# The gated delta rule of a two-block model: packed 64x64 blocks, worked beside the projections

## The reference, cut to what matters

```
q, k, v = split(silu(causal_dwconv(concat(q, k, v), conv_w)))       # 4 taps
beta = sigmoid(b);  g = -exp(a_log) * softplus(a + dt_bias)
q = l2norm(q) * 128 ** -0.5;  k = l2norm(k)
gcum = cumsum of g in each chunk of 64;  decay[t, s] = exp(gcum[t] - gcum[s]) for s <= t, else 0
N = -(strictly lower part of (beta k) k^T * decay)
T = I + N;  P = N
for _ in range(5):  P = P @ P;  T = T + T @ P
w = T @ (beta k exp(gcum));  u = T @ (beta v)
attn = q k^T * decay;  q_g = q exp(gcum);  k_g = k exp(gcum[last] - gcum)
for each chunk c (in order):                                        # the scan
    v_new = u - w @ S;  o = q_g @ S + attn @ v_new;  S = S * exp(gcum[last]) + k_g^T @ v_new
y_a = rmsnorm(o) * norm_w * silu(z)
```

## Time and profile before

| what | value |
|---|---|
| median of three runs | 2964.35 us |
| the profiled execution's own time | 2963.22 us |
| its span, first to last instruction | 2961.3 us |
| TensorE busy | 2835.7 us, 96% of the span |
| VectorE (DVE) busy | 1564.7 us, 53% |
| ScalarE (ACT) busy | 841.1 us, 28% |
| GpSimd (POOL) busy | 206.2 us, 7% |
| granted TensorE clock, mean | 0.983 of full speed |

### The profile page before, as it was taken

How to read it: one execution, slowest core, us unless ns; L and a number is a source line. 1 busy time by engine, 2 the same in 40 slices (tenths; PEclk the granted TensorE clock), 3 DMA queues, 4 the chain that set the end, 5 groups by cost and what they waited for, 6 DMA issues and landing times.

```text
span 2961.3 us, 31843 instructions
## 1 busy us (share of the span) xinstructions
PE 2835.7 (96%) x12912; PEld 2303.7 (78%) x12912; DVE 1564.7 (53%) x1824; ACT 841.1 (28%) x870; POOL 206.2 (7%) x182
## 2 busy tenths in 40 slices
PE   7999998899999997899989999999999999999997
PEld 6777776688777776778777888888888888888887
DVE  6456454683543567562465545445454544445458
ACT  4335244552421232222232122212222122222122
POOL 3003000160000000001040000000000000000004
PEclk9999999999999999899999999999999999999999
DMA  5224311242222220022232222222222222222232
GB/s 196 72 71 171 121 58 57 102 173 100 92 87 85 75 90 35 1 111 88 99 128 86 100 99 87 100 100 100 92 95 100 100 100 88 97 101 100 97 147 85
DMA packets 44379, 287.52 MB, mean 97 GB/s; under 512 B 5136, under 2 KB 9360, under 8 KB 10432
## 3 DMA queue, kind: packets, MB, share of 16 engines
q1 hardware_dynamic: 39616, 260.06, 24.0%
q0 software_dynamic: 4320, 24.85, 2.2%
q10 hardware_dynamic: 288, 0.43, 0.0%
HBM read 268.54 MB, written 16.78 MB: 96 GB/s over the span
## 4 chain that ended last, share of the span: by engine, by line
PE 87%; DVE 8%; ACT 3%; issue 1%; POOL 0%; DMA 0%; DVEq 0%; SPq 0%; ACTq 0%; POOLq 0%
PE ps L1135 10%; PE ps L1137 10%; PE ps L1136 10%; PE ps L610 9%; PE ps L612 9%; PE ps L611 9%; PE ps L1153 5%; PE ps L1152 5%; PE ps L1151 5%; PE ps L1059 2%; PE ps L1061 2%; PE ps L1060 2%; PE ps L949 1%; DVE w_lo L1708 1%; ACT w_hi L1205 1%
## 5 line engine op out<-in xcount | busy, mean ns | idle before, releaser
L1708 DVE TENSOR_TENSOR w_lo<-raw,w_hi 128x2048 fp32r<-128x2048 f32 x228 | 529.3, 2322 | 538.4 <-ACT w_hi L1205 528.6
L1205 ACT ACTIVATE w_hi<-raw 128x2048 fp32r<-128x2048 f32 x227 | 434.5, 1915 | 1224.6 <-PE ps L1137 478.1
L610 PE MATMUL ps<-h_hi,w_hi 128*128 128x512 f32 x1216 | 495.2, 407 | 17.3 <-DVE h_lo L1713 15.5
L1135 PE MATMUL ps<-h_hi,w_hi 128*128 128x512 f32 x1280 | 499.7, 390 | 6.5 <-DVE w_lo L1708 4.1
L1137 PE MATMUL ps<-h_hi,w_lo 128*128 128x512 f32 x1280 | 499.0, 390 | 0.0
L1136 PE MATMUL ps<-h_lo,w_hi 128*128 128x512 f32 x1280 | 498.9, 390 | 0.0
L612 PE MATMUL ps<-h_hi,w_lo 128*128 128x512 f32 x1216 | 477.1, 392 | 0.0
L611 PE MATMUL ps<-h_lo,w_hi 128*128 128x512 f32 x1216 | 477.0, 392 | 0.0
L610 PEld LDWEIGHTS ps<-h_hi,w_hi 128*128 128x128 f32 x1216 | 230.5, 190 | 74.8 <-issue 26.2
L1135 PEld LDWEIGHTS ps<-h_hi,w_hi 128*128 128x128 f32 x1280 | 241.0, 188 | 58.3 <-DVE w_lo L1708 4.5
L1137 PEld LDWEIGHTS ps<-h_hi,w_lo 128*128 128x128 f32 x1280 | 240.9, 188 | 50.3
(11 more groups left out here) (408 smaller groups left out, 3136.5 us busy)
## 6 DMA issues: line engine op xcount, KB each, us to landing
raw<-weights SPq DMA_DIRECT2D x232, 1024.0 KB, 4.8
x_spill<-X POOLq DMA_DIRECT2D x8, 1024.0 KB, 7.1
X<-x_in SPq DMA_DIRECT2D x4, 1024.0 KB, 10.8
x_res<-x_in SPq DMA_DIRECT2D x4, 1024.0 KB, 7.4
x<-X POOLq DMA_DIRECT2D x4, 1024.0 KB, 4.6
x_res<-x SPq DMA_DIRECT2D x4, 1024.0 KB, 7.8
X<-x_spill POOLq DMA_DIRECT2D x4, 1024.0 KB, 9.4
x_back<-x_spill POOLq DMA_DIRECT2D x4, 1024.0 KB, 9.0
```

The source lines that it names most:

```text
L610: pe.matmul(o, w_hi[:, s % 2, w], h_hi[:, t, :], start=(t == 0), stop=False)
L1135: pe.matmul(o, w_hi[:, s % 2, w], h_hi[:, t, :], start=(t == 0), stop=False)
L1205: A(w_hi[:, slot, :], raw[:, slot, :], ACT.Copy).then_inc(w_hi_ready, 1)
L1708: V.tensor_tensor(w_lo[:, slot, :], raw[:, slot, :], w_hi[:, slot, :].bitcast(F32), ALU.subtract).then_inc(w_ready, 1)
```

## The change

- The 16 units take a `beat`, and one generator `delta_rule` issues the whole preparation on TensorE between the k-tiles of v (beats 64 to 95) and of z (96 to 127). The copies and elementwise steps move into the lists of ACT and DVE beside these units. No loop over `pair` stands behind the projections any more.
- Head i and head i + 2 are packed: the 64 tokens of a chunk of one lie on partitions 0 to 63, those of the other on 64 to 127. A product over blocks is 16 matmuls of 64x64 by 64x64 for two heads (j = 0 and j = 1 on the two halves of the rows), all in one bank (`packed`). Silu writes q, k and v in that packed order.
- The transposed powers are computed by a product of their own in place of a transpose, and both are copied by ACT.
- The l2 norms are not applied to the tiles. The sums are taken per token (`l2_sums`: 32 matmuls with one moving column), and the factors of q and k go into per-token vectors (`token_factors`), which are spread over rows with an identity as moving operand (`spread`).
- The scan handles four heads in 64-row halves of bank 4 (w by state), banks 5 and 6 (k_g by v_new), makes outputs per chunk of 64 tokens, and multiplies by a copy of attn that is zero in the other head's half. POOL zeroes it after the last unit, and ACT copies into it. Silu of z moves behind ACT's rounding of eight tiles in the scan.

The core of the diff on TensorE:

```
             def turn_ba():
-                for tt in range(4):
-                    mm = pe.transpose(ps[:, 5, 8 * tt:8 * tt + 8], ba_rows[:, 128 * tt:128 * tt + 128], ident[0:8, 0:8])
+                for c in range(8):
+                    for j in range(2):
+                        mm = pe.matmul(ps[64 * j:64 * j + 64, 5, 4 * c:4 * c + 4], ba_rows[:, 64 * c:64 * c + 64], ...)
+            def packed(o, lhs, rhs):
+                for c in range(8):
+                    x = slice(64 * c, 64 * c + 64)
+                    for j in range(2):
+                        r = slice(64 * j, 64 * j + 64)
+                        mm = pe.matmul(o[r, x], lhs[r, x], rhs[r, x], start=True, stop=True)
+            def delta_rule(beat):
+                yield from beat.until(68)
+                sum_gates()
+                yield from beat.until(75)
+                pe.wait_ge(sem("g_sums_read"), 1)
+                for i in range(2):
+                    spread(ps[:, 4 + i, :], g_sums, i).then_inc(full[4 + i], 1)
+                yield from beat.until(84)
+                l2_sums(1)
...
+                for it in range(5):
+                    for i in range(2):
+                        yield from beat.until(97 + 4 * it + i)
+                        pe.wait_ge(read[6 + i], C_PT + it - 1)
+                        pe.wait_ge(read[4 + i], F_P + 2 * it - 1)
+                        packed(ps[:, 4 + i, :], nt_pow[:, i, :], n_pow[:, i, :]).then_inc(full[4 + i], 1)
+                        if it < 4:
+                            packed(ps[:, 6 + i, :], n_pow[:, i, :], nt_pow[:, i, :]).then_inc(full[6 + i], 1)
...
+                    for i in range(2):
+                        yield from beat.until(99 + 4 * it + i)
+                        pe.wait_ge(sem("inv_ready"), i + 1)
+                        pe.wait_ge(read[4 + i], F_INV + 2 * it - 1)
+                        packed(ps[:, 4 + i, :], n_pow[:, i, :], inv_t[:, i, :]).then_inc(full[4 + i], 1)
...
             for n in range(4):
                 for s in range(4):
-                    project_unit(U_QKVZ, G_QKVZ, n, s, 32)
+                    project_unit(U_QKVZ, G_QKVZ, n, s, 32, beat=beat)
...
-            for pair in range(2):
...
+            def scan_output(c, h):
+                o = ps[:, 7 if c // 2 % 2 else 0, 128 * h + 64 * (c % 2):128 * h + 64 * (c % 2) + 64]
+                pe.matmul(o, v_new[:, c % 2, 128 * (h % 2):128 * (h % 2) + 128], attn_z[:, h, 64 * c:64 * c + 64], start=True, stop=False)
+                pe.matmul(o, state[:, c % N_STATES, hs], tokens_at(Q_T, h % 2, c)[:, 64 * (h // 2):64 * (h // 2) + 64], start=False, stop=True)
```

On ACT and DVE, cut to what stands beside which unit:

```
                     if (n, s) == (2, 1):
+                        silu_conv(1)
+                        l2_squares(1)
+                        exp_decay()
+                        take_l2()
+                    if (n, s) == (3, 0):
+                        take_powers(0)
+                        take_powers(1)
+                    if (n, s) == (3, 1):
+                        take_powers(2)
+                        take_powers(3)
+                        silu_conv(2)
...
+                    if (n, s) == (2, 2):
+                        token_factors()
+                        first_powers()
...
                     if (n, s) == (3, 0):
                         dve.wait_ge(bank_free, G_QKVZ + 6 + 2)
+                        conv_taps(2, (0,))
+                        add_power(0)
+                        conv_taps(2, (1,))
+                        add_power(1)
```

More of the change, by code:

```diff
@@ L451, in two_blocks_kernel @@
         dve_order, act_order, pool_order = sem("dve_order"), sem("act_order"), sem("pool_order")
+        full = {b: sem(f"bank{b}_full") for b in range(4, 8)}
+        read = {b: sem(f"bank{b}_read") for b in range(4, 8)}
         block = ctx.enter_context(nc.Block())
@@ new lines, in products, with turn_blocks @@
+            def products(o, a, b, i):
+                for c in range(8):
+                    for j in range(2):
+                        r = slice(64 * j, 64 * j + 64)
+                        mm = pe.matmul(o[r, 64 * c:64 * c + 64], tokens_at(a, i, c)[:, r], tokens_at(b, i, c)[:, r],
+                                       start=True, stop=True)
+                return mm
+            def turn_blocks(b, base, i, half):
+                for c in range(4 * half, 4 * half + 4):
+                    mm = turn(ps[:, b, 128 * (c % 4):128 * (c % 4) + 128], tokens_at(base, i, c))
+                mm.then_inc(full[b], 1)
@@ L936, in _ @@
                         pe.wait_ge(sem("group_root"), 3)
[L937 to L950, removed]
@@ L952, in _ @@
-            for pair in range(2):
[L953 to L1010, removed]
[L1011 to L1018 removed]
+                        l2_sums(0)
@@ new lines, in take_w_and_u @@
+            def take_w_and_u():
+                for i, (b0, use) in enumerate(((6, C_W), (4, F_W))):
+                    for j in range(2):
+                        act.wait_ge(full[b0 + j], use)
+                        A(w_t[:, 2 * i + j, :], ps[:, b0 + j, :], ACT.Copy).then_inc(read[b0 + j], 1)
+                for i, (b0, use) in enumerate(((6, C_U), (4, F_U))):
+                    for half in range(2):
+                        act.wait_ge(full[b0 + half], use)
+                        A(proj[:, V_T + i + 2 * half, PAD:], ps[:, b0 + half, :], ACT.Copy).then_inc(read[b0 + half], 1)
@@ new lines, in take_k @@
+            def take_k(i):
+                b0, use = ((6, C_K), (4, F_K))[i]
+                for half in range(2):
+                    dve.wait_ge(full[b0], use)
+                    dve.wait_ge(full[b0 + 1], use)
+                    cols = slice(8 * i + 4 * half, 8 * i + 4 * half + 4)
+                    V.tensor_tensor(b128(k_be[:, 2 * i + half, :]), b128(ps[:, b0 + half, :]), bc(be[:, cols], 128), ALU.mult)\
+                     .then_inc(sem("k_taken"), 1)
+                    V.tensor_tensor(b128(proj[:, KEY_T + i + 2 * half, PAD:]), b128(ps[:, b0 + half, :]), bc(kgs[:, cols], 128), ALU.mult)\
+                     .then_inc(read[b0 + half], 1)
```

518 lines of the change are left out of this document (323 added, 195 removed).

## The result

The changed kernel takes 2934.08 us (median of four runs, 2932.28 to 2938.03) against 2964.59 us (four runs, 2963.48 to 2964.89): a ratio of 0.990, 95% interval 0.9882 to 0.9917. The forecast was 2938 us, range 2905 to 2972. The profiled execution took 2934.05 us.

What follows compares the result with a forecast made beforehand. TensorE was taken as the bound, busy 96% of the span with 87% of the chain. Removing preparation, adding its matmuls between k-tiles, a later scan start and a shorter scan: 2963.2 - 104.7 + 84.1 + 2.5 - 6.8 = 2938.3 us, range 2905 to 2972.

Steps and rivals of the forecast that it cites:

- signs for "right": Stage some 84 us longer, no preparation behind it, groups of 1.2 to 1.7 us, scan of 31 us at clock 1.0.
- Stage beside the projections: Preparation's matmuls between k-tiles of the v and z units: 84.1 us added, for 104.7 us of preparation removed.
- narrow group: Group of 16 matmuls, 64 rows, 64 weight columns, N = 64, between k-tiles: 1.4 us each, 36 groups, 50.4 us.
- pair row: First layer's scores: two matmuls on different 64-row halves, a pair started every 0.11 us; taken as the lower bound.
- the wait at beat 68: TensorE waits for DVE's gates soon after the v units begin: 1 us (0 to 3).
- the changes of the array: Switches between split and whole array around groups: 0.1 us each way, 32 places, 6.4 us (3.2 to 6.4).
- Wide groups: Six groups for the spread of q's factor, w and u: 1.9 us each, 11.4 us (10.8 to 25).
- Rival (c): Ten places in the powers each wait 1.5 us for a copy; 15 us return, 2953 us; chance 0.12.
- Rival (a): The two row halves, writing one bank, do not work at once: 2.2 us a group of 16, 2982 us; chance 0.18.
- Rival (b): Row halves overlap fully, 0.9 to 1.0 us a group of 16 between k-tiles: 2910 us; chance 0.20.
- The scan: Scan at full clock with chunks of 3.7 to 4.2 us: 31 us against 37.8, a gain of 6.8 (3 to 9).
- The start of the scan: After the last unit, DVE's tiles, POOL's zeroing and ACT's copies: 3.2 us in place of 0.7, +2.5 (1 to 3).

Runs made afterwards that it cites:

- e5: Changed kernel with each of the 28 groups of the powers issued twice, same products into the same places: 2957.97 us.
- e4: Changed kernel with the 16 matmuls in packed() reordered, all eight of the upper rows first, then all eight of the lower: 2952.27 us.
- e8: Changed kernel with three extra unused matmuls behind the first k_g by v_new alone, the gap before the first chunk left empty: 2917.23 us.
- e2: Changed kernel with POOL's zeroing moved to when unit (3, 2) is done, and ACT's copies into attn_z before it takes w and u: 2930.44 us.
- e7: Changed kernel with two extra unused matmuls before the scan's first chunk alone, zeroing unchanged: 2935.02 us.
- e10: Changed kernel with the l2 sums of q issued two matmuls at a time between the k-tiles at beats 69 to 76: 2937.24 us.
- e1: Changed kernel with ten extra unused matmuls at the scan's start: four before the first chunk, six behind the first k_g by v_new: 2916.11 us.
- e3: Changed kernel with POOL's zeroing early and extra unused matmuls, four before the first chunk and three behind the first k_g by v_new: 2912.63 us.
- e6: Changed kernel with POOL's zeroing early and fewer extra unused matmuls, two before the first chunk, one behind the first k_g by v_new: 2915.02 us.
- e11: Changed kernel with POOL's zeroing early, extra unused matmuls in both gaps (two and two) and the l2 sums of q spread between k-tiles: 2928.60 us.
- e12: Changed kernel with POOL's zeroing early, no filler before the first chunk, two extra unused matmuls behind the first k_g by v_new: 2916.20 us.
- e9: Kernel before the change with five extra unused matmuls in its own gaps around the start of the scan: 2952.33 us.

## Why the prediction was right

The time, the direction and the main mechanism (preparation out, its matmuls between the k-tiles, no waits there) came out as forecast. But two terms were wrong and nearly cancelled, so that the number is within 4 us is luck: against the 2938.3 forecast for the profiled execution, the stage beside the projections cost 15.4 us less, the start of the scan 1.2 less and the scan 18.0 more, and the part behind the stage, where nothing was changed, came out 5.6 shorter. Of the signs for "right" in the prediction, groups of 1.2 to 1.7 us and a scan of 31 us at a clock of 1.0 did not come.

- *Stage beside the projections.* Forecast +84.1, measured +68.7, of which 1.0 had come in ahead of the stage. The step that failed is the price of the narrow group: 1.4 us where it is 0.93, 36 x 0.47 = 17 us. I had taken the middle between the pair row and a pace of issue that no row showed; the pair row's half, 0.9, was near the value. The other misses nearly cancel: the products (4 at 0.93 and not 1.9) cost 4 us less, turning b and a 1.5 less (1.03 us where it was 0.34), the wait at beat 68, forecast at 1 us, did not come; against that the changes of the array cost 0.36 us a place and not 0.2, some 5 more for 32 places, and the clock behind the l2 sums some 3 more.
- *Wide groups*: 1.9 forecast, 1.8 measured.
- *Waits in the powers*: TensorE has none in the trace from 1062 to 1204 us. Rival (c) is out, and e5 shows it from the other side.
- *Rival (a), halves in turn*: out, by e4: a group costs 1.6 to 1.7 us only when it is issued in turn, and even with 28 of them so the stage (318.6) is 5 us shorter than before (323.7).
- *Rival (b), full overlap*, forecast 2910: its price for the groups was right, its time not, because of the scan.
- *The scan*, forecast 31 us at a clock of 1.0, measured 49.0 at 0.5. This step failed outright. I reasoned that TensorE comes out of dense k-tiles, and left out what I had worked out a paragraph above: some 3 us of waits for POOL and ACT at the start, in which TensorE has next to nothing. At the lower level a chunk costs 6.0 us; e8 has 29.0 us for the scan with that gap filled, so the forecast of 31 was near for a clock that stays up.
- *The start of the scan*: the first matmul 1.98 us after the tiles are taken, 2.0 forecast. The second chunk waits 2.89 us, where 1.21 are left in e2 without POOL's zeroing and ACT's copies there: 1.7 us late from these, 1.2 forecast.

Two readings in the prediction are off without weight: it writes 1135.56 for 1135.59 in the 104.7 us, and takes the old l2 sums at 3.5 us, where the next k-tile stands 3.03 us behind their start (the new ones cost 1.5 us more in all, 1.6 forecast).

Sum by measured terms, stage only: -104.7 + 68.7 + 1.3 (the scan's first matmul 1.98 us after the tiles are taken, before 0.69 after u) + 11.2 = -23.5, which is the difference of the low parts.

## What to carry to other kernels

Small products that use half the rows can be issued pairwise on the two halves between the k-tiles of a dense projection at little over half the price, also into one bank if the partitions differ; the order of issue alone decides (0.93 against 1.6 to 1.7 us for 16). When a stage becomes thin at its start, look at the granted clock of the whole stage behind it: here 2.6 us of useless matmuls in one wait were worth 17 us (e8). Compare stages from a point ahead of the edit, not by times from the profile's start alone: in e4 that was 4 of 23.5 us. Before work is moved out of a place, look for whose lateness it was covering there.

## What the runs showed of the hardware

- A chain of small matmuls without a gap can stay at the lower level of the clock. The same scan, 100% busy by the records from its second chunk on, ran at 1.2 GHz but for its first 0 to 6 us in six kernels (changed, e2, e4, e5, e7, e10) and at 2.4 GHz to its end in e1, e3, e6, e8, e11, e12, depending on the gaps at its start (the 0.91 from 1220 to 1238 in e8 is a fall behind the scan, which ends at 1233.4: 1228 to 1234 has 1.00). It is no rule for all small matmuls: the old scan came back to 1.00 in its course.
- At full clock the new scan's chunk takes 3.3 us, from 1219.3 to 1222.6 in e1's chain, where I had 3.95: the instructions of the outputs, with 64 columns, start every 0.11 to 0.14 us, and k_g by v_new on two row halves takes 0.65.
- The part behind the stage is the same code in all kernels and took 1645.0 to 1658.4 us from the low part to the end of the span. It doesn't follow the edits: 1653.3 before, 1647.7 changed, 1646.1 in e3, 1653.4 in e8, 1645.0 in e9, 1658.4 in e11. The part ahead of the stage scatters too: the projection of b and a starts between 983.5 (e8) and 989.4 us (e4). In the kernel before, the first segment of the feed-forward loop, from its first matmul to the first of its down projection, took 94.2 us (1576.0 to 1670.2) against 88.3 in all others. So up to 13 us of a difference between two profiles of this kernel behind the stage, and up to 6 ahead of it, can be no effect of a change, and what separates medians by less than 5 us (e3, e6, e12) stays open. The forecast's bound of 0.2% for what a measurement can tell was too narrow for single runs.
- An extra float32 matmul of 128x512 is two instructions and takes 0.86 us at full clock; I had reckoned 0.43 for e1.
